# The MLP's down product as seven half-size products, token-major, with weight sums on GpSimd

## The reference, cut to what matters

```python
D_FF = 4 * D_MODEL                                   # 4096
...
        x = x + merged @ w_out[l]
        h2 = rms_norm(x, norm_mlp[l])
        x = x + jnp.square(jax.nn.relu(h2 @ w_up[l])) @ w_down[l]
    return rms_norm(x, norm_final)
```

## Time and profile before

| what | value |
|---|---|
| time, median of 3 runs (lowest to highest) | 1131.48 us (1131.18 to 1131.64) |
| profiled execution, first to last instruction (span) | 1129.3 us |
| TensorE busy / VectorE / ScalarE / GpSimd | 99% / 57% / 46% / 14% of the span |
| share of TensorE in the chain that ended last | 88% |
| TensorE clock granted | 0.998 of full speed |

### The profile page before, as it was taken

The page is one execution under the profiler, slowest core; times in us unless marked ns, Lnnn a source line. Parts: engine busy times, 40 slices in busy tenths (PEclk is TensorE's granted clock), DMA queues, the critical chain, the costliest instruction groups (busy, mean ns, idle before and its releaser), DMA issues.

```text
span 1129.3 us, 14393 instructions
## 1 busy us (share of the span) xinstructions
PE 1118.0 (99%) x5336; PEld 886.7 (79%) x5336; DVE 642.8 (57%) x1093; ACT 519.2 (46%) x909; POOL 160.9 (14%) x198
## 2 busy tenths in 40 slices
PE   9999999999999999999999999999999999999997
PEld 6787787887677788767778888888888888888886
DVE  7787977887668674465454545555443333544232
ACT  6656567465666544244344433335433212333131
POOL 2022111320323221022121200021000000000021
PEclk9999999999999999999999999999999999999999
DMA  6322323332111123211322122223223232223212
GB/s 227 113 75 93 97 90 100 106 111 86 55 48 68 57 93 103 93 57 56 113 75 94 68 82 95 102 84 112 93 93 112 79 108 93 94 95 111 93 57 75
DMA packets 31270, 103.28 MB, mean 91 GB/s; under 512 B 3552, under 2 KB 5984, under 8 KB 31200
## 3 DMA queue, kind: packets, MB, share of 16 engines
q1 hardware_dynamic: 30624, 101.74, 26.4%
q10 hardware_dynamic: 576, 0.62, 0.2%
HBM read 99.72 MB, written 2.10 MB: 90 GB/s over the span
## 4 chain that ended last, share of the span: by engine, by line
PE 88%; DVE 6%; ACT 4%; issue 2%; DMA 1%; SPq 0%; POOL 0%; DVEq 0%; ACTq 0%; POOLq 0%
PE ps L754 26%; PE ps L756 25%; PE ps L755 25%; PE ps L877 3%; PE ps L892 3%; PE ps L923 2%; DVE wl L1262 2%; DVE xs L1341 1%; PE ps L917 1%; DVE sg L1357 1%; DVE cc L1373 1%; DMA xt<-xT 1%; ACT wh L956 1%; ACT aa L1031 0%; ACT cc L1044 0%
## 5 line engine op out<-in xcount | busy, mean ns | idle before, releaser
L754 PE MATMUL ps<-xgh,wh 128*128 128x512 f32 x847 | 336.7, 398 | 1.2 <-issue 0.7
L756 PE MATMUL ps<-xgh,wl 128*128 128x512 f32 x847 | 330.2, 390 | 0.0
L755 PE MATMUL ps<-xgl,wh 128*128 128x512 f32 x847 | 329.9, 390 | 0.0
L1262 DVE TENSOR_TENSOR wl<-raw,wh 128x1024 fp32r<-128x1024 f32 x180 | 230.9, 1284 | 137.8 <-ACT wh L956 137.4
L956 ACT ACTIVATE wh<-raw 128x1024 fp32r<-128x1024 f32 x180 | 188.4, 1049 | 127.7 <-PE ps L756 127.1
L754 PEld LDWEIGHTS ps<-xgh,wh 128*128 128x128 f32 x847 | 159.1, 188 | 39.0 <-issue 6.7
L756 PEld LDWEIGHTS ps<-xgh,wl 128*128 128x128 f32 x847 | 159.0, 188 | 33.8
L755 PEld LDWEIGHTS ps<-xgl,wh 128*128 128x128 f32 x847 | 159.2, 188 | 32.5 <-issue 1.0
L1738 POOL TENSOR_SCALAR Pt<-Pt,stat 128x256 f32<-128x256 f32 (+2 forms) x128 | 75.1, 599 | 274.0 <-DVE stat L1519 198.9
L754 PE MATMUL ps<-fh,wh 128*128 128x512 f32 x240 | 93.4, 389 | 0.0
L755 PE MATMUL ps<-fl,wh 128*128 128x512 f32 x240 | 93.4, 389 | 0.0
(11 more groups left out here) (232 smaller groups left out, 1579.0 us busy)
## 6 DMA issues: line engine op xcount, KB each, us to landing
raw<-wst SPq DMA_DIRECT2D x180, 512.0 KB, 3.5
bst<-nbias SPq DMA_DIRECT2D x8, 256.0 KB, 3.4
xt<-xT SPq DMA_DIRECT2D x3, 512.0 KB, 7.6
outT<-ot SPq DMA_DIRECT2D x2, 384.0 KB, 2.5
outT<-ot SPq DMA_DIRECT2D x6, 128.0 KB, 2.0
cstt<-cst SPq DMA_DIRECT2D x1, 448.0 KB, 5.3
raw<-wst SPq DMA_DIRECT2D x1, 320.0 KB, 4.6
xt<-xT ACTq DMA_DIRECT2D x1, 256.0 KB, 3.4
```

What stands on the lines that cost most here:

```text
L754: e.matmul(o, high, a, start=(k == 0), stop=False)
L755: e.matmul(o, high, b, start=False, stop=False)
L756: e.matmul(o, low, a, start=False, stop=stop).then_inc(tile_done, 1)
L1262: e.tensor_tensor(wl_t[:, u % NHL, :], raw_t[:, u % NRAW, :], f32(wh_t[:, u % NHL, :]), ALU.subtract).then_inc(lo_done, 1)
```

## The change

Each round of hidden features is multiplied as a 2x2 block product in the Winograd form of Strassen's scheme: seven products in place of eight. The MLP now runs in 4 rounds. A round has 8 up chunks (64 tiles, as before in kind) and then 14 "form" units of 4 tiles (56 tiles, where 64 were). The product is now token-major: the stationary operand is a 128x128 piece of fh or fl (128 hidden features by 128 tokens), the moving one 512 output columns of a weight sum, and a bank holds 128 tokens by 512 features. Tokens 0-255 and 256-511 are the block rows, hidden features of a pair of up chunks the block columns, output columns 0-511 and 512-1023 the block columns of w_down.

- Activations: for each pair of up chunks VectorE forms four sums `fs` (256 wide), and the high and low parts hold 7 forms (`fh`, `fl`, KH = 4 pairs by 7 forms by 256 tokens) in two pieces each: forms 0 to 2, then 3 to 6.
- Weights: SyncE loads the four quarters of w_down (b11, b12, b22, b21, two buffers each, 8 loads of 512 KB a round) and GpSimd makes the sums T1 = b12 - b11 (in t14), T3 = b22 - b12 (in b12), T2 = b22 - T1 (in b11), T4 = b21 - T2 (in t14): 8 sums of 128x1024 a round. Each is split into high and low like any unit.
- Outputs: `ADDS` says which blocks of the residual each product goes to, with which sign: 20 additions of 128x512 a round in place of 16 in a half of the MLP. To save additions the blocks 12 and 21 of the residual are kept less block 22 until the last round ("folds").
- Layout: x is turned to token-major once, with 32 TensorE transposes (`turn_x`) in the first round, copied by ScalarE and (less block 22) by VectorE.
- End: the final norm is a sum along rows, by ScalarE with its accumulator (`row_norms`), and the gain is applied along rows from a broadcast load `fin`. The split last chunk, its matmuls with ones and the sums on GpSimd are gone.

```diff
+PARTS = ("P1", "P5", "P1", "P5", "P6", "P6", "P3", "P3", "P7", "P7", "P2", "P2", "P4", "P4")
+REGION = {"P1": (0, 1), "P5": (2, 3), "P6": (4, 5), "P3": (0, 1), "P7": (2, 3), "P2": (4, 5), "P4": (0, 1)}
...
+ADDS = {"P1": (("11", 1), ("22", 1)), "P5": (("22", 1), ("21", -1)), "P6": (("22", 1),), "P3": (("12", 1),),
+        "P7": (("22", 1), ("12", -1)), "P2": (("11", 1),), "P4": (("21", 1),)}
...
+        for n, p in enumerate(PARTS):
+            kk = PARTS[:n].count(p)
+            for s in range(2):
...
+                for k in (2 * kk, 2 * kk + 1):
+                    self.tiles.append((name, k, k == KH - 1))
...
-    for hf in range(2):
-        ch.seq([("up", hf, c) for c in range(16)], KD, 2, 7)
-        ch.seq([("dn", hf, j) for j in range(KD)], 16, 4, 13)
+    for r in range(ROUNDS):
+        names = [("up", r, c) for c in range(2 * KH)]
...
+        ch.downs(r)
...
+                UNIT_AT[u] = max(ch.units[u - NHL][2] + 2.0, UNIT_AT[u - 1] + 3.2)
...
+            def down_tile(name, k, high, low, stop):
+
+                _, r, p, s = name
+                n = 2 * (KH * r + k) + (1 if FORM[p] < 3 else 2)
+                q.wait_ge(fh_done, n)
+                q.wait_ge(fl_done, n)
+                a, b = fh[:, k, FORM[p], blk(s)], fl[:, k, FORM[p], blk(s)]
+                o = bank[ch.bank[name]]
+                e.matmul(o, a, high, start=(k == 0), stop=False)
+                e.matmul(o, a, low, start=False, stop=False)
+                e.matmul(o, b, high, start=False, stop=stop).then_inc(tile_done, 1)
...
+            def turn_x():
...
+                    for n in (s, 2 + s):
+                        for j in range(KD):
+                            done = e.transpose(bank[2 * (n // 2) + j // 4][:, blk(j % 4)], xt[:, j, blk(n)], ident)
...
+            def row_norms():
...
+                    q.wait_ge(half_sum, i)
+                    q.wait_ge(nb_done, 4)
+                    e.activation(ssq, xtok[:, n, 512:1024], ACT.Square, accum_out=stat[:, 0, n:n + 1]).then_inc(half_sum, 1)
...
+            def pairs(r, k):
...
+                e.tensor_tensor(fs[:, 0, :], a21, a22, ALU.add).then_inc(fs_done, 1)
+                e.tensor_tensor(fs[:, 1, :], a11, a21, ALU.subtract).then_inc(fs_done, 1)
...
+                e.tensor_tensor(fs[:, 2, :], fs[:, 0, :], a11, ALU.subtract).then_inc(fs_done, 1)
...
+                e.tensor_tensor(fs[:, 3, :], a12, fs[:, 2, :], ALU.subtract).then_inc(fs_done, 1)
...
+                e.tensor_tensor(fl[:, k, 0:3, :], fa[:, pair % 2, 1:4, :], f32(fh[:, k, 0:3, :]), ALU.subtract).then_inc(fl_done, 1)
...
+                e.tensor_tensor(fl[:, k, 3:7, :], fs[:, :, :], f32(fh[:, k, 3:7, :]), ALU.subtract).then_inc(fl_done, 1)
...
+            def row_gains():
...
+                    q.wait_ge(half_sum, 3 + n)
+                    q.wait_ge(fold_done, 4)
...
+            def weight_sums():
...
+                    for kk in range(2):
+                        v = form_no[r, "P1", kk]
+                        yield UNIT_AT[v] + 4.0
+                        q.wait_ge(t1_done, 2 * r + kk + 1)
+                        unit_split(q, v)
+                        e.tensor_tensor(b11[:, kk, :], b22[:, kk, :], t14[:, kk, :], ALU.subtract).then_inc(t2_done, 1)
+                    for kk in range(2):
+                        v = form_no[r, "P5", kk]
+                        yield UNIT_AT[v] + 8.0
+                        q.wait_ge(t2_done, 2 * r + kk + 1)
+                        q.wait_ge(b_in[21][kk], 16 * (r + 1))
+                        unit_split(q, v)
+                        e.tensor_tensor(t14[:, kk, :], b21[:, kk, :], b11[:, kk, :], ALU.subtract).then_inc(t4_done, 1)
```

More of the change, by code:

```diff
@@ L18 @@
 NHL = 4
+KH = 4
+ROUNDS = 4
 BIG = 1.0e30
@@ L231, in build @@
         sb("gap", [128, 592])
+        xs_ = ExitStack()
+        b21, t14 = (sb(n, [128, 2, 1024], F, xs_) for n in ("b21", "t14"))
+        xs_.close()
         xt = sb("xt", [128, KD, S])
@@ L383, in build @@
         DRV_ALL = 8
+        UP_AT = [ch.units[form_no[r, "P1", 0] - 2 * KH][1] for r in range(ROUNDS)]
+        DN_END = [end["dn", r, "P4", 1] + 1 for r in range(ROUNDS)]
         ev_at, last = {}, 0.0
@@ L584, in weights @@
             def weights():
-                for u in range(wst.shape[0]):
-                    if u == 0:
+                for w in range(wst.shape[0]):
+                    if w == 0:
                         yield -75
@@ L633, in stores @@
                 yield 5000
[L634 to L646, removed]
+                for n in (2, 3, 0):
+                    q.wait_ge(out_dve, {2: 2, 3: 4, 0: 5}[n])
+                    if n == 0:
+                        q.wait_ge(out_act, 1)
+                    e.dma_start(out[:, n, :], xtok[:, n, :]).then_inc(out_done, 16)
+                q.wait_ge(out_dve, 6)
+                e.dma_start(out[:, 1, 0:512], xtok[:, 1, 0:512]).then_inc(out_done, 16)
+                q.wait_ge(out_done, 16 * 5)
+            merge([weights(), starts(), biases(), swaps(), downs(), gains(), stores()])
         @block.tensor
@@ new lines, in acc_, with differ_x @@
+            def acc_(name, s):
+                row, half = PLACE[name]
+                return xtok[:, row + s, 512 * half:512 * half + 512]
+            def differ_x():
+                for s in range(2):
+                    for n, name in enumerate(("21", "12")):
+                        yield UP_AT[0] + (19.0, 29.0)[s] + n
+                        q.wait_ge(xtok_done, 2 * s + 1)
+                        q.wait_ge(xturn_done, 2 * s + n + 1)
+                        e.tensor_tensor(acc_(name, s), bank[3 * n], acc_("22", s), ALU.subtract).then_inc(xd_done, 1)
@@ new lines, in downs @@
+            def downs(r, p, s):
+                name = ("dn", r, p, s)
+                yield ev_at[name]
+                q.wait_ge(tile_done, end[name] + 1)
+                q.wait_ge(xtok_done, 4)
+                q.wait_ge(xd_done, 4)
+                if r == FINAL and p == "P4":
+                    q.wait_ge(fold_done, 3 + s)
+                for acc, sign in ADDS[p]:
+                    q.wait_ge(ev_done, ch.added[name, acc][0])
+                    e.tensor_tensor(acc_(acc, s), acc_(acc, s), bank[ch.bank[name]], ALU.add if sign > 0 else ALU.subtract).then_inc(ev_done, 1)
@@ L1846, in weight_stream, with down_weights @@
     add_seq(tiles(a["w_out_2"][0]), 4, 7)
-    up, down = tiles(a["w_up_2"][0]), tiles(a["w_down_2"][0])
-    for hf in range(2):
-        add_seq(up[16 * hf:16 * hf + 16], 2, 7)
-        add_seq(down[:, 16 * hf:16 * hf + 16], 4, 13)
+    add(tiles(a["w_up_2"][0])[:2, :7])
+    add(tiles(a["w_up_2"][0])[:2, 7:])
+    add(tiles(a["w_up_2"][0])[2:])
     s = np.stack(order)
     return np.ascontiguousarray(s.reshape(-1, UT, 128, 128).transpose(0, 2, 1, 3).reshape(-1, 128, UT * 128))
+def down_weights(w):
+    w = w.reshape(ROUNDS, 2, 2, 2, 128, 2, 512)
+    units = []
+    for r in range(ROUNDS):
+        for row, col, kk in ((0, 0, 0), (0, 1, 0), (0, 0, 1), (0, 1, 1), (1, 1, 0), (1, 1, 1), (1, 0, 0), (1, 0, 1)):
+            units.append(w[r, kk, :, row, :, col].transpose(1, 0, 2).reshape(128, 1024))
+    return np.ascontiguousarray(np.stack(units))
 def params(a):
```

451 lines of the change are left out of this document (274 added, 177 removed).

## The result

The changed kernel takes 1120.33 us in the median of its runs (1119.95 to 1120.69), the kernel before 1131.45 (1131.18 to 1131.64). The ratio is 0.9902 with a 95% interval of 0.9889 to 0.9915: 11.1 us faster, where 12.0 was forecast (1119.5 us, range 1112.0 to 1127.5).

The account below looks back on a forecast made before the run. TensorE was taken as the bound, busy 1118.0 of 1129.3 us. Saving, transposes, down stages and end: -21.7 + 3.7 + 5.2 + 0.8 = -12.0 us, span 1117.3, time 1119.5 us, range 1112 to 1127.5.

Parts of the forecast that it names:

- The saving: TensorE's down tiles go from 256 to 224, three 512-column matmuls each at 0.2255 us: 21.7 us less.
- The transposes: 32 added TensorE transposes in two groups of 16, the second waiting for nothing: 3.7 us more.
- The down stages: TensorE waits for low parts at the start of each of four down stages: 1.3 us a round, 5.2 in all.
- P: Time of one GpSimd sum of 128x1024, taken as 2.7 us, twice the median of the 512-wide sum.
- 3P - 6.8: Stall per round at a down stage's start if VectorE goes before the second T4 sum: 1.3 us.
- the rival in which the cover holds: GpSimd sums shorter than 2.27 us, so no stall at the down stages: 1114.3 us, chance 0.22.
- the step on DMA: 32 weight loads of 512 KB cost nothing, and stay free if a load is 10 us late.
- Who goes first: At the down stages VectorE's first fl was taken to go before GpSimd's second T4 sum, which then holds the second fl.
- the rival of 2.9 us a round: GpSimd goes first at the down stages, delaying the first fl: 11.6 us in all, 1125.9 us, chance 0.15.
- The end: TensorE stalls 0.8 us before the last four tiles; the whole end costs 0.8 us more than before.
- The sum: All terms together: -21.7 + 3.7 + 5.2 + 0.8 = -12.0 us, a span of 1117.3 us.

Follow-up runs that it names:

- e8: Changed kernel with the late T4 sums of e2, the end order of e4 and the early transposes of e7 together: 1111.57 us.
- e6: Kernel before with 14 tiles in place of 16 in each down chunk, an eighth of the down product left out: 1110.65 us.
- e1: Changed kernel without GpSimd's weight sums; P4 to P7 take a loaded quarter of w_down instead: 1114.49 us.
- e4: Changed kernel with the last round's end reordered: folds and gains behind the last weight split, row squares 0 and 1 first, P4's additions before scaled row 3: 1118.34 us.
- e7: Changed kernel with the two groups of transposes 6 and 8 tiles earlier, and their copies earlier too: 1118.62 us.
- e2: Changed kernel with each round's T4 sums waiting until the last pair's low parts are written: 1115.15 us.
- e5: Changed kernel with each T4 sum made twice, the same values written again: 1136.43 us.
- e3: Changed kernel with the last pair's low parts ahead of the split of P5's second unit at each down stage's start: 1117.06 us.

## Why the prediction was right

*The saving.* 96 matmuls x 0.2255 = 21.7 us. Right: where nothing stalls the token-major tiles start at the same spacing (178 in 40 us in e8), and e6 measured 21.0 for the same tiles alone.

*The transposes.* 3.7 forecast. Two groups of 16 took 1.66 and 1.67 us, with 0.1 behind each: 3.5. (The forecast had read 0.1 too, and put 0.15 into the sum.) The second group waited for nothing. The page's row for them:

```profile
L921 PE MATMUL ps<-cstt,xt 128*128 128x128 f32 x32 | 3.8, 272 | 0.0
```

*The down stages.* 5.2 forecast, 6.4 measured (e1 gives 5.8 by time). The place, the two operations and the cause were right; that the sum is near is luck, from two errors that offset. P was 2.4 and not 2.7 us. With it 3P - 6.8 gives 0.4 a round, which is what the second and third cost (0.43 and 0.41), and by that the forecast would have been 1.6 for the stages and 1115.9 us in all. The rival in which the cover holds asked for sums below 2.27 us and missed by 0.13. And the rounds are not alike, which I had taken them to be: the first cost 4.3, of which 2.5 is a wait, 1.6 the slow matmuls behind it and the rest the restart. That step failed: I had counted each round from an idle VectorE and had noted neither that the first sums wait for the transposes nor what four sums in a row leave behind. The lower clock behind a stall was in no term. The fourth cost 1.25: its second T2 started 1.9 us ahead of the last chunk's reading, 0.8 later than in rounds two and three, behind the second T1 sum that its load had released sooner. The traces of the changed kernel, e4 and e7 have nine rounds behind the first with this order of queues: in five the first fl of the round's first pair took 0.95 us, and the excess is 0.41 to 0.43; in four it took 3.16, and the excess is 1.24 to 1.42. No run moved a load on purpose. So the step on DMA ("free", even 10 us late) left out that a load which lands sooner moves the sums too.

*Who goes first.* VectorE's first fl started some 0.25 us ahead of the second T4 sum in every round, the second fl was the one stretched, and the rival of 2.9 us a round is out.

*The end.* 0.8 forecast on balance: ahead of the last four tiles 0.8, measured 0.64 (0.55 in the gap, the rest in the slower start behind it); from TensorE's last matmul to the end 9.9 forecast, 10.0 measured. Both sides of the balance hold, and e4 shows that the order of VectorE's queue was behind it.

*The sum.* -21.7 + 3.5 + 6.4 + 0.8 = -11.0, with 0.4 us more that the changed kernel's profiled run lost before 302 us, where nothing is changed (the same matmul of the first block's norm stands at 302.31 for 301.94): -10.6 for -10.4 of span.

## What to carry to other kernels

GpSimd was no free engine beside VectorE here: time it took was time in which VectorE's operations with two SBUF inputs stood still, so look for what on the critical path VectorE has to deliver in that stretch, and put the GpSimd work behind it. A cost that is four times the same in a schedule should be worked out for the first round by itself, with what delays its first inputs, and a round should be tried with its loads a microsecond sooner as well as late. Where queues run in order, look last at what stands ahead of the final work on each: reordering alone gave 2.0 us at the end here (2.6 in the trace) and 8.8 in all, beside 11.1 for the change itself.

## What the runs showed of the hardware

- GpSimd against VectorE, by operation: in the changed kernel an fs operation of 0.42 us took up to 2.63 and an fl of 1.22 took 3.43 beside a sum; a split of 1.22 took 2.24 in e2 and 3.42 in e5. The additions with a PSUM input kept 0.67 to 0.69 us in e2, where five of them ran wholly beside the late T4 sums of the second round. GpSimd's own sum of 2.4 us was stretched to 2.96 when VectorE's operation had begun before it.
- Behind TensorE's stalls of 2.50 us (changed kernel, first round), 2.59 and 4.65 us (e5, last and first) matmuls ran at a granted clock of 0.50, 0.427 us apart, for seven or eight of them (1.4 to 1.6 us lost). Behind those of 1.23 (e7), 1.35 (e3) and 1.74 us (e5, twice) it stayed 1.00.
